# Serialising the three indirect scatters of each finished expert on the GpSimd queue (one-layer MoE decoder step, one Trainium2 core)

## What is computed

```python
logits = h @ w_router + b_router              # (544, 32)
top_v, top_i = top_k(logits, 4)
gates = softmax(top_v)
for each of the 32 experts e, for the rows x of h routed to e:
    g = min(x @ w_gate[e] + b_gate[e], 7)
    u = clip(x @ w_up[e] + b_up[e], -7, 7)
    y = ((u + 1) * g * sigmoid(1.702 * g)) @ w_down[e] + b_down[e]
    ffn[token] += gate * y                    # four experts per token
out = rmsnorm(x + g2 * ffn)
```

## Time and profile before

| What | Value |
|---|---|
| Time before, median of 3 runs | 1336.98 us (1334.65 to 1338.87) |
| Profiled execution, span on the core | 1348.8 us |
| Profiled execution, time around the span | not given by the page |
| PE busy | 1287.5 us, 95% of the span |
| DVE busy | 517.3 us, 38% |
| POOL busy | 242.2 us, 18% |
| ACT busy | 90.2 us, 7% |
| Data moved | 487.60 MB, mean 362 GB/s |
| The 90 scatters (L1402) | 90.0 us busy on POOL, 1000 ns each |
| The 90 gathers of the loop (L1391) | 91.3 us busy on POOL, 1014 ns each |

### The profile page before, as it was taken

How to read it: one execution, slowest core, us unless ns; L and a number is a source line. 1 busy time by engine, 2 the same in 40 slices (tenths; PEclk the granted TensorE clock), 3 DMA queues, 4 the chain that set the end, 5 groups by cost and what they waited for, 6 DMA issues and landing times.

```text
span 1348.8 us, 32006 instructions
## 1 busy us (share of the span) xinstructions
PE 1287.5 (95%) x14057; PEld 744.1 (55%) x14057; DVE 517.3 (38%) x813; ACT 90.2 (7%) x165; POOL 242.2 (18%) x315
## 2 busy tenths in 40 slices
PE   4999999779999999999999999999999999999997
PEld 2787754514655655555554555544555555555674
DVE  1213213542333444444433333333334444444446
ACT  3200011200000000000000000000000000000002
POOL 4001300062111111111122221111111111111110
PEclk9999999789999999999999999999999999999999
DMA  9885960356999999999999999999999999999993
GB/s 327 256 327 212 346 246 32 149 224 248 411 410 423 405 413 407 409 410 405 421 407 411 411 416 410 407 408 409 425 417 406 400 421 407 416 401 424 418 411 154
DMA packets 64294, 487.60 MB, mean 362 GB/s; under 512 B 11911, under 2 KB 21607, under 8 KB 38917
## 3 DMA queue, kind: packets, MB, share of 16 engines
q1 hardware_dynamic: 47442, 455.92, 83.2%
q0 software_dynamic: 11264, 19.96, 4.1%
q10 hardware_dynamic: 5555, 11.25, 2.3%
HBM read 468.41 MB, written 25.97 MB: 367 GB/s over the span
## 4 chain that ended last, share of the span: by engine, by line
PE 93%; DVE 2%; issue 2%; DMA 2%; ACT 1%; SPq 0%; POOL 0%; DVEq 0%; POOLq 0%; ACTq 0%
PE acc L1877 52%; PE acc L1900 23%; PE acc L945 9%; PE acc L989 4%; PE acc L862 2%; DMA raw<-in_w_ada 1%; PE acc L1981 1%; PE acc L1000 1%; PE acc L880 1%; ACT h_t L488 1%; PE acc L1997 0%; DVE picked L1593 0%; PE acc L961 0%; DMA rows<-h_rows,row_first 0%; DVE raw_b L1586 0%
## 5 line engine op out<-in xcount | busy, mean ns | idle before, releaser
L1877 PE MATMUL acc<-raw_b,ht 128*32 128x512 f32 x3024 | 381.2, 599 | 16.4 <-issue 13.0
L1877 PE MATMUL acc<-raw,ht 128*32 128x512 f32 x2928 | 339.0, 592 | 0.0
L1877 PEld LDWEIGHTS acc<-raw_b,ht 128*32 128x32 f32 x3024 | 142.0, 111 | 235.1 <-issue 231.2
L1650 DVE TENSOR_TENSOR g_sb<-acc,bias_gu 128x768 f32<-128x768 f32 x32 | 30.6, 957 | 570.4 <-PE acc L1877 570.4
L1877 PEld LDWEIGHTS acc<-raw,ht 128*32 128x32 f32 x2928 | 151.6, 110 | 156.6 <-issue 149.8
L1391 POOL DMA_INDIRECT rows<-h_rows,row_next x90 | 91.3, 1014 | 742.1 <-DVE row_next L1542 722.7
L1900 PE MATMUL acc<-raw_b,at 128*32 128x256 f32 x2976 | 183.7, 379 | 0.0
L1900 PE MATMUL acc<-raw,at 128*32 128x256 f32 x2976 | 183.7, 379 | 0.0
L1900 PEld LDWEIGHTS acc<-raw_b,at 128*32 128x32 f32 x2976 | 135.7, 110 | 42.2 <-issue 9.8
L1900 PEld LDWEIGHTS acc<-raw,at 128*32 128x32 f32 x2976 | 133.5, 109 | 32.1
L945 PE MATMUL acc<-h_t,raw 128*128 128x288 f32 (+1 forms) x512 | 118.3, 393 | 1.1 <-DVE h_t L702 1.1
(11 more groups left out here) (249 smaller groups left out, 639.8 us busy)
## 6 DMA issues: line engine op xcount, KB each, us to landing
raw<-in_w_down SPq DMA_DIRECT2D x33, 2048.0 KB, 15.5
raw<-in_w_gate SPq DMA_DIRECT2D x31, 2048.0 KB
raw<-in_w_up SPq DMA_DIRECT2D x31, 2048.0 KB
raw_b<-in_w_gate SPq DMA_DIRECT2D x31, 2048.0 KB
raw_b<-in_w_up SPq DMA_DIRECT2D x31, 2048.0 KB
raw_b<-in_w_down SPq DMA_DIRECT2D x31, 2048.0 KB
raw<-in_w_ada SPq DMA_DIRECT2D x24, 1024.0 KB, 12.1
expert_rows<-zeros ACTq DMA_DIRECT2D x1, 8704.0 KB, 30.4
```

The source lines that it names most:

```text
L1650: dve.tensor_tensor(g_sb[:, :, :], gate_of(i, 0), plus(0), ALU.add).then_inc(g_read, 1)
L1877: mm = pe.matmul(gu_of(i)[b][q * TB:(q + 1) * TB, :].rearrange("p (m n) -> p m n", m=2), ht_of(i)[:, b, k, :], w[:, kk, :, q * CW:(q + 1) ...
```

## The change

Between the three scatters of one expert, POOL now waits. Before the second it waits until `y_stored` has counted the landing of the first, before the third until it has counted the second. Inside the hardware loop, where the expert's number is a register, an empty instruction (`nop`) follows each wait, as it does before the first scatter already. Nothing else is changed: the same transfers with the same indices, and the waits on `y_stored` of SP, ACT and DVE, stay as they are.

```diff
                     for b in range(SB):
+                        if b:
+                            pool.wait_ge(y_stored, 16 * (SB * e + b))
+                            if not isinstance(e, int):
+                                pool.nop(nofuse=True)
                         pool.indirect_dma_start(y_quarter, bass.IndirectOffsetOnAxis(ap=y_idx[:, b:b + 1], axis=0),
                                                 y_sb[:, b, :], None, bounds_check=Q * ROWS - 1, oob_is_err=False)\
                             .then_inc(y_stored, 16)
```

## The result

The changed kernel took **1323.21 us** (median of 4 runs, 1320.95 to 1324.97), the kernel before beside it 1337.38 (4 runs, 1334.65 to 1338.87): ratio 0.9892, interval 0.9877 to 0.9907. The forecast was 1337.5 in a range from 1330 to 1343, so it was wrong; the case that came is rival B, at half its price.

The account below looks back on a forecast made before the run. The prediction took the loop to run at PE's pace, with DMA keeping up. Loop 0 and tail +0.5 us on the profiled span of 1348.8, less the 11.8 us difference to the timed runs, gave 1337.5 us, range 1330 to 1343.

Parts of the forecast that it names:

- rival B: Loop: PE's gaps go with the burst of six indirect issues, up to 26 us less, 1311; half gives 1324; chance 0.13.
- The loop's waits cost 0: Loop: added waits fall into POOL's 24 us sleep, next gather has 6.8 us to spare, so cost 0.
- PE's gaps, "I take 0": Loop: moving the scatters leaves PE's gaps unchanged, taken as 0, with bounds of 0.9 us a step less or more.
- the step of 31.0 us had the same six POOL issues: Loop: argument against rival B, that a 31.0 us step had six issues in it and PE busy throughout.
- unprofiled runs are 11.8 us shorter, which suggests that part of the gaps belongs to the profiling: Loop: argument against rival B, from the profiled span of 1348.8 us against the runs' median of 1336.98.
- The tail, +0.5 us: Expert 29's serial scatters end 12.4 us later, at 1305.3; read-back loads keep 0.7 and 0.5 us spare; 0.5 added for a miss.
- the lone 7.1: Tail: expert 29's first scatter, with no gather ahead, landed 7.1 us after issue; used for each of its three scatters.
- the loads' time: Tail: SP's two read-back loads, issued at 1305.3 to an empty queue, land at 1311.9 and 1316.8.
- L1593 not behind a DMA: Tail: sign to show in the changed profile, that the rows of L1593 do not wait for a transfer.
- Rival A: Tail: lone scatters of 9 to 10.4 us make the read-back the bound, +5 to +9.3 us, 1342 to 1346; chance 0.13.

Follow-up runs that it names:

- again_c: The kernel before, unchanged, profiled once more on chip 4, which has gaps: 1341.6 us, mean step 31.55 us.
- paced_b: Kernel before plus two POOL memsets between third gather and first scatter, no wait on landings, on chip 12: 1324.30 us, ratio 0.9799.
- again: The kernel before, unchanged, timed and profiled again on chip 8, which has no gaps: 1314.57 us over 19 runs, step 30.96 us.
- third_only_b: Kernel before with a wait ahead of the third scatter alone, on chip 4: 1322.16 us, ratio 0.9853.

## Why the prediction was wrong

**The loop's waits cost 0: right.** The next gather had 8.2 us to spare where 6.8 were forecast, and DVE's wait ahead of g_sb is 17.1 us. The changed kernel's steps are 30.96 us in the first comparison and on chip 3, where the kernel before has them too.

**PE's gaps, "I take 0": this step failed.** The bounds were 0.9 us a step to either side, and the lower bound came: 0.95 in the profile, 14.2 us over the whole kernel in the timed runs. Two arguments held it at 0. First, "the step of 31.0 us had the same six POOL issues". The count was right and the pitch was not read: I took two windows and a number of instructions, where POOL in order of time shows 1.40 us ahead of the third. Read so, the one step with six issues and no loss was the one with a pause, which is evidence for rival B. Second, that "unprofiled runs are 11.8 us shorter, which suggests that part of the gaps belongs to the profiling". The runs since don't bear this out. Every execution here, timed or profiled, lies 1.7 to 1.9 us over its own span (`again_c`: span 1339.9, time 1341.6, and the timed runs beside it 1340.5 to 1343.7). By that the profiled execution of before took 1348.8 + 1.8 = 1350.6 us, which is what chip 12 shows in timed runs: it was one that lost more, and its loss is real time. Whether it ran on another chip than the timed ones, the record does not say. The difference of 11.8 us was itself a sign that the loss varies.

**The tail, +0.5 us: right in its mechanism, low by half.** Expert 29's scatters after:

```profile
1255.78 0.98 POOL L1406 DMA_INDIRECT expert_rows<-y_sb,y_idx  x1 [10.67 <-DVE y_sb L1585]
1263.33 0.98 POOL L1406 DMA_INDIRECT expert_rows<-y_sb,y_idx  x1 [6.57 <-DMA expert_rows<-y_sb,y_idx]
1271.03 0.98 POOL L1406 DMA_INDIRECT expert_rows<-y_sb,y_idx  x1 [6.73 <-DMA expert_rows<-y_sb,y_idx]
```

They are 7.6 and 7.7 us apart, where 7.9 were forecast; this line's landings in that stretch are 6.3, 6.8 and 6.9 us (min, median, max), against the lone 7.1. They are far from the 2.3 us that the prediction estimated from the figures of the Trainium skill, "DMA: Bandwidth & Descriptors" (anatomy of one DMA). SP read back at 1277.36, its loads landed 8.0 and 14.0 us later. The mis-sized term is the loads' time: 6.6 and 11.5 were forecast, so the second took 2.5 us more. SP itself issued them 1.3 us earlier than forecast (5.3 us behind the last g_sb row instead of 6.6), and 0.5 were to spare: 2.5 - 1.3 - 0.5 = 0.7, near the 1.01 that DVE waits. The sum left out SP's next load (L1346): it was issued at 1278.21, 0.4 us behind the second, where in before it came 5.4 us behind. That it shares the engines with the two is likely the reason for the longer loads, but was not tried. DVE's two rows:

```profile
1285.96 2.28 DVE L1597 TENSOR_TENSOR picked<-picked 128x2048 f32<-128x2048 f32 x1
...
1291.77 2.29 DVE L1597 TENSOR_TENSOR picked<-picked 128x2048 f32<-128x2048 f32 x1 [1.01 <-DMA picked<-expert_rows]
```

My test "L1593 not behind a DMA" fails by this row, at 1.01 us. Rival A's price, 5 us and more, did not come: none of expert 29's scatters took the 8.7 us it needed. They and the read-back now stand on the chain that ended last, with 1.5% and 1.1% of the span.

**Rival B: right as a mechanism, at a price that depends on the chip.** It put 0.9 us on 29 steps, 26 us. The profiles give 28.4 in the loop, the timed runs of the first comparison 14.2 in all, and 18 to 26 us of time for the kernels without the run on chips 4 and 12 (1341.45 - 1322.97, 1350.71 - 1324.30). On four of the six chips of the experiments the price is 0. The chance of 0.13 was too small for a rival whose pattern stood in the rows read.

## What to carry to other kernels

Where PE has gaps that no semaphore explains, lay the other engines' rows in order of time beside a step that has none, and compare the distances, not the counts. A run of indirect DMAs issued back to back can cost TensorE time on some chips and nothing on others, so time such a kernel on more than one chip. Here a pause of some 2 us within the run was enough, as was a wait that was free anyway. Waits on landings are worth having only off the path: here they are free in the loop and cost 1 us ahead of the read-back.

## What the runs showed of the hardware

**Two kinds of chip.** On chips 8, 3, 15 and 11 the kernel before takes 1314.0 to 1314.8 us, on 4 and 12 it takes 1341.5 and 1350.7. The granted clock does not set them apart: its mean is 0.98 to 0.99 in every execution. Each chip was visited once, so whether the chip or its state at the time makes the difference is not shown. A part of it lies ahead of the loop and stays when the loop's loss is gone: the kernels without that loss take 1322 to 1324 us on chips 4 and 12. There, beside `gate_up(0)`, POOL issues three gathers and 20 scatters in a row (L1419 of before), 1.3 us apart on both kinds. `paced_b` has its first g_sb row 17.0 us later than `again` (321.12 and 304.12), its third only 6.2 us later (372.68 and 366.46), mostly because PE waits 8.5 us for DVE ahead of that one in `again`. The same window (columns as above), `paced_b` and then `again`:

```profile
289.00:316.00 27.00, 19.30 (x70) 4.17 (x68) 9.28 (x19) 0.00 (x0) 15.83 (x16) 0.87 0.33 121
```
```profile
289.00:316.00 27.00, 27.00 (x256) 7.58 (x252) 16.54 (x28) 0.84 (x1) 19.14 (x19) 1.00 0.96 387
```

In the same 27 us PE ran 70 matmuls against 256, and the DMA engines moved 121 against 387 GB/s. PE's loss looks like the loop's at large. The fall of the transfers does not show that they are slowed too: SP issues a load only when PE has read what its slots held, and in `paced_b` it issued none for 27 us:

```profile
285.32 0.33 SPq L1319 DMA_DIRECT2D raw_b<-in_w_gate  x1
312.42 0.33 SPq L1319 DMA_DIRECT2D raw_b<-in_w_up  x1
```

In the loop the weights' own packets are slower: between 371 and 1264 us, 2.4% of those of 16 KB took over 900 ns in before and 1.5% in `again_c`, but 0.3% in `again` and, on the chip of `again_c`, in `third_only_b`. Instructions fetched by DMA are not what PE lacks in the loop: before has no packet of that kind from 390 to 1310 us.

**Lost records.** On the chips with the loss the trace lacks landing records of the gathers: before has 980 of 1536, after 1479; chips without it have 1509 to 1536. But `third_only_b` (1148) and `paced_b` (1015) lack hundreds too and lose no time in the loop, so the missing records are a mark of such a chip and not the measure of the loss.

**Left open:** what the run of issues takes from PE on these chips, why five in a row cost nothing and six do, why the later place makes the loss smaller, and what sets the chips apart. No run here shows it.
